# A two-block FFN kernel: the upper part of gate and up weights times both parts of the rows in one product of 512 columns

## The reference, cut to what matters

```python
h = rmsnorm(x, norm_ffn)                      # x: 256 x 1024
x = x + (silu(h @ w_ffn_gate) * (h @ w_ffn_up)) @ w_ffn_down
return rmsnorm(x, norm_final)                 # D_FF = 2816 = 22 tiles of 128
```

## Time and profile before

| | |
|---|---|
| runs | 1421.64, 1420.68, 1421.60 us; median 1421.6 us |
| profiled execution | 1421.5 us, of which its span (first to last instruction) is 1419.7 us |
| busy over the span | PE 77%, PEld 44%, DVE 26%, ACT 21%, POOL 22% |
| chain that ended last | DMA 56%, PE 40% of the span |
| mean granted TensorE clock | 0.893 of full speed |

### The profile page before, as it was taken

One profiled execution on the slowest core, in us unless ns is written; L12 is line 12 of the kernel. 1 busy time (PEld: TensorE's weight loads), 2 busy tenths in 40 slices (PEclk: granted clock), 3 DMA queues, 4 the chain that ended last, 5 costly groups with the idle time before them and its releaser, 6 DMA issues.

```text
span 1419.7 us, 19641 instructions
## 1 busy us (share of the span) xinstructions
PE 1090.4 (77%) x8358; PEld 631.5 (44%) x8358; DVE 366.5 (26%) x723; ACT 304.8 (21%) x449; POOL 312.2 (22%) x216
## 2 busy tenths in 40 slices
PE   7999997656757666666685675666678999999998
PEld 7998732111311211211131121121125987999997
DVE  6686530000100001000010010100004856453343
ACT  5753210000000000000000000000004637454443
POOL 6896000000000000000000000000003787286661
PEclk9999999878777888687877888888799999999999
DMA  9513999999999999999999999999999943475540
GB/s 288 187 34 121 379 426 427 428 427 427 427 428 428 428 428 428 428 429 428 428 428 429 428 428 428 429 428 429 428 427 337 226 137 119 156 246 178 178 149 31
DMA packets 95288, 478.06 MB, mean 337 GB/s; under 512 B 11098, under 2 KB 64217, under 8 KB 70393
## 3 DMA queue, kind: packets, MB, share of 16 engines
q1 hardware_dynamic: 94528, 476.30, 83.4%
q10 hardware_dynamic: 697, 0.84, 0.2%
HBM read 475.88 MB, written 1.25 MB: 336 GB/s over the span
## 4 chain that ended last, share of the span: by engine, by line
DMA 56%; PE 40%; DVE 2%; issue 1%; ACT 1%; SPq 0%; DVEq 0%; ACTq 0%
PE bank L1325 21%; DMA ring<-in_expert_w_up 20%; DMA ring<-in_expert_w_gate 18%; DMA ring<-in_expert_w_down 18%; PE bank L2120 4%; PE bank L1024 4%; PE bank L1046 2%; PE bank L410 1%; PE bank L887 1%; PE bank L427 1%; PE bank L423 1%; DMA cst<-in_shape_consts 0%; PE bank L442 0%; PE bank L438 0%; DVE work L1979 0%
## 5 line engine op out<-in xcount | busy, mean ns | idle before, releaser
L1024 PE MATMUL bank<-ring,work 128*32 128x512 f32 x2000 | 304.2, 741 | 203.1 <-DMA ring<-in_expert_w_up 125.5
L1024 PEld LDWEIGHTS bank<-ring,work 128*32 128x32 f32 x2000 | 60.4, 122 | 436.4 <-DMA ring<-in_expert_w_up 202.6
L1299 POOL TENSOR_TENSOR slot_r<-ring,slot_r 128x512 fp32r<-128x512 f32 (+1 forms) x123 | 227.8, 1880 | 106.8 <-ACT slot_r L1271 106.8
L1308 POOL TENSOR_TENSOR slot_r<-ring,slot_r 128x512 fp32r<-128x512 f32 x16 | 21.9, 1396 | 956.2 <-ACT slot_r L1277 956.2
L1046 PE MATMUL bank<-ring,work 128*32 128x512 f32 x1024 | 154.7, 739 | 80.6 <-DMA ring<-in_expert_w_down 76.4
L1325 PE MATMUL bank<-slot_r 128*128 128x256 f32 (+2 forms) x1080 | 159.5, 287 | 3.8 <-DVE tokm_r L2482 1.8
L1325 PEld LDWEIGHTS bank<-slot_r 128*128 128x128 f32 (+1 forms) x1080 | 144.3, 191 | 7.9 <-issue 5.1
L1098 DVE TENSOR_TENSOR work<-work,bank 128x512 f32<-128x512 f32 x16 | 11.0, 688 | 490.4 <-PE bank L1024 490.4
L1325 PE MATMUL bank<-work_r,slot_r 128*128 128x256 f32 x704 | 129.1, 283 | 0.2 <-DVE chan_r L1847 0.2
L1108 DVE SCALAR_TENSOR_TENSOR hres<-bank,work,hres 128x512 f32<-128x512 f32 x64 | 48.1, 751 | 269.9 <-PE bank L1061 266.9
L1271 ACT ACTIVATE slot_r<-ring 128x2048 fp32r<-128x2048 f32 x62 | 116.6, 1902 | 3.2 <-DMA ring<-in_w_in 3.0
(11 more groups left out here) (418 smaller groups left out, 1045.8 us busy)
## 6 DMA issues: line engine op xcount, KB each, us to landing
ring<-in_expert_w_down SPq DMA_DIRECT2D x64, 2048.0 KB, 35.6
ring<-in_expert_w_gate SPq DMA_DIRECT2D x63, 2048.0 KB, 36.0
ring<-in_expert_w_up SPq DMA_DIRECT2D x62, 2048.0 KB, 35.8
ring<-in_w_in SPq DMA_DIRECT2D x23, 1024.0 KB, 8.2
ring<-in_w_ffn_gate SPq DMA_DIRECT2D x11, 1024.0 KB, 6.1
ring<-in_w_ffn_up SPq DMA_DIRECT2D x11, 1024.0 KB, 5.3
ring<-in_w_ffn_down SPq DMA_DIRECT2D x11, 1024.0 KB, 5.3
ring<-in_w_out SPq DMA_DIRECT2D x8, 1024.0 KB, 4.9
```

Of the source, the lines that this page charges most:

```text
L1024: ins = pe.matmul(bank[b][32 * j:32 * j + 32, :], xg[:, 2 * s + kk, a * CAP:(a + 1) * CAP], w_[kk][:, j * W5:(j + 1) * W5], start=(s == 0 ...
L1299: ins = eng.tensor_tensor(ring_r[s][:, a:a + step], ring[:, s, a:a + step], ring_r[s][:, a + UNIT:a + UNIT + step].bitcast(F32), ALU.subtract)
L1308: ins = eng.tensor_tensor(ring_r[s][:, at:at + q], ring[:, s, at:at + q], ring_r[s][:, at + UNIT:at + UNIT + q].bitcast(F32), ALU.subtract)
```

## The change

1. The upper and lower parts of the rows now lie side by side in `early` (`x3[:, k, 0]`, `x3[:, k, 1]`). A step k is `both_parts`: weights upper x both parts, 512 columns over a whole bank, and weights lower x rows upper, 256 columns into its first half. The second half of a bank holds weights upper x rows lower.
2. So the two halves must be added. For gate and for up, ScalarE copies the second half from PSUM to SBUF (`ffw`), VectorE adds the first half from PSUM to it. Then VectorE multiplies gate by rs, and silu by up; both multiplications now read SBUF alone. A new semaphore `ff_half` counts the copies.
3. Tile 2 has its sums in banks 1 and 2 in place of 4 and 6, and does not wait for `ff_h`; down 0 waits for `ff_h` >= 3 before its first product into bank 1.
4. The final norm's weights are loaded into `flatc`; the semaphores `hn_ready` and `repeat_ready` become one, `pool_made`.

The diff's core (what is left out are the semaphores of point 4 and calls of `upper_parts` and `lower_parts` with the new places):

```diff
-        nf2_bc = poolT[:, :, :].rearrange("p a t -> p (a t)")
+        nf2_bc = flatc[:, 0:D]
...
-        xh = ftile(5, 4, True).rearrange("p (k t) -> p k t", k=DK)
+        x3 = early_r[:, :].rearrange("p (k a t) -> p k a t", k=DK, a=2)
+        ffw = (work(5), work(6))
+
+        def gate_bank(u):
+
+            return 1 if u == 2 else 4 + u % 2
+
+        def up_bank(u):
+
+            return 2 if u == 2 else 6 + u % 2
...
                         for i in range(3):
                             for half in range(2):
+                                if g + f + t + i == 0 and half:
+                                    pe.wait_ge(S.ff_h, 3)
                                 ins = part(f, t, half, (i,))
                 ins.then_inc(S.ff_down_out, 1)
+
+            def both_parts(out_, wh, wl, k):
+
+                pe.matmul(out_[:, :], wh, x3[:, k].rearrange("p a t -> p (a t)"), start=k == 0, stop=False, skip_group_check=True)
+                return pe.matmul(out_[:, 0:T], wl, x3[:, k, 0], start=False, stop=k == DK - 1, skip_group_check=True)
...
-                        ins = three(pe, bank[b][:, 0:T], (w_[0][:, k, 0:P], w_[1][:, k, 0:P]), (xh[:, k, :], chan_r[:, k, :]),
-                                    k == 0, k == DK - 1)
+                        ins = both_parts(bank[b], w_[0][:, k, 0:P], w_[1][:, k, 0:P], k)
...
-                    if u >= 2:
+                    if u > 2:
                         pe.wait_ge(S.ff_h, u - 1)
...
-                            ins = three(pe, bank[b + u % 2][:, 0:T], (wh[:, k, cols_], wl[:, k, cols_]),
-                                        (xh[:, k, :], chan_r[:, k, :]), k == 0, k == DK - 1)
+                            ins = both_parts(bank[b], wh[:, k, cols_], wl[:, k, cols_], k)
...
             for u in range(NFT):
                 g, f = u // FB, u % FB
-                act.wait_ge(S.ff_scaled, u + 1)
+                act.wait_ge(S.ff_g_out, u + 1)
                 if u >= 2:
                     act.wait_ge(S.ff_h, u - 1)
+                act.activation(ffw[u % 2][:, 0:T], bank[gate_bank(u)][:, T:2 * T], ACT.Copy).then_inc(S.ff_half, 1)
+                act.wait_ge(S.ff_scaled, u + 1)
                 act.activation(ffs[u % 2], ffg[u % 2], ACT.Silu).then_inc(S.ff_silu, 1)
+                act.wait_ge(S.ff_u_out, u + 1)
+                act.activation(ffw[u % 2][:, T:2 * T], bank[up_bank(u)][:, T:2 * T], ACT.Copy).then_inc(S.ff_half, 1)
                 act.wait_ge(S.ff_h, u + 1)
...
-                dve.tensor_tensor(ffg[u % 2], bank[4 + u % 2][:, 0:T], rs3_bc, ALU.mult).then_inc(S.ff_scaled, 1)
+                dve.wait_ge(S.ff_half, 2 * u + 1)
+                link(dve.tensor_tensor(ffg[u % 2], ffw[u % 2][:, 0:T], bank[gate_bank(u)][:, 0:T], ALU.add))
+                dve.tensor_tensor(ffg[u % 2], ffg[u % 2], rs3_bc, ALU.mult).then_inc(S.ff_scaled, 1)
...
                 scaled_gate(u)
+                dve.wait_ge(S.ff_half, 2 * u + 2)
+                upper = ffw[u % 2][:, T:2 * T]
+                link(dve.tensor_tensor(upper, upper, bank[up_bank(u)][:, 0:T], ALU.add))
                 dve.wait_ge(S.ff_silu, u + 1)
-                dve.wait_ge(S.ff_u_out, u + 1)
                 if f == 0 and g >= 2:
                     dve.wait_ge(S.ff_down_out, g - 1)
-                dve.tensor_tensor(h_full(g)[:, f], ffs[u % 2], bank[6 + u % 2][:, 0:T], ALU.mult).then_inc(S.ff_h, 1)
+                dve.tensor_tensor(h_full(g)[:, f], ffs[u % 2], upper, ALU.mult).then_inc(S.ff_h, 1)
```

More of the change, by code:

```diff
@@ L169, in build @@
         cst = sb("cst", [P, max(KEEP_W, MASKS_AT + SLOT // 2)])
-        early = sb("early", [P, SLOT])
+        early, early_r = sb_r("early", [P, SLOT])
         qk = early[:, 0:4 * W5].rearrange("p (a h t) -> p a h t", a=2, h=H)
@@ L1168, in mix1_wout @@
             sp.dma_start(rw, io["router_w"].rearrange("o (k p) e -> (o p) k e", p=P)).then_inc(S.wab_in, 16)
-        sems("hn_ready rel_in relrow_out relrow_stored")
-        sems("repeat_ready rows2_evac")
+        sems("pool_made rel_in relrow_out relrow_stored")
+        sems("rows2_evac")
         sems("proj2_out proj2_evac dots_out relu_ready relu_used mask_ready biasmask_ready")
@@ L1549, in second_pe @@
             pe.wait_ge(S.rows2_evac, 2)
-            pe.wait_ge(S.repeat_ready, 1)
+            pe.wait_ge(S.pool_made, 2)
             pe.matmul(bank[1][:, 0:T], repeat, kgw[0:IDX_DIM, :], start=True, stop=True)
@@ L1668, in second_act @@
                 if t == 0:
-                    act.wait_ge(S.hn_ready, 1)
+                    act.wait_ge(S.pool_made, 1)
                 else:
@@ L1793, in second_pool @@
             pool.wait_ge(S.scat_added, 4 * E - 1)
-            pool.tensor_tensor(tokm[:, 0], hres[:, 0], nf_bc, ALU.mult).then_inc(S.hn_ready, 1)
+            pool.tensor_tensor(tokm[:, 0], hres[:, 0], nf_bc, ALU.mult).then_inc(S.pool_made, 1)
             pool.wait_ge(S.slot_used, E * SPE)
@@ L1797, in second_pool @@
             pool.tensor_copy(repeat.rearrange("p (r c) -> p r c", r=4),
-                             ident[0:IDX_DIM, 0:IDX_DIM].unsqueeze(1).to_broadcast([IDX_DIM, 4, IDX_DIM])).then_inc(S.repeat_ready, 1)
+                             ident[0:IDX_DIM, 0:IDX_DIM].unsqueeze(1).to_broadcast([IDX_DIM, 4, IDX_DIM])).then_inc(S.pool_made, 1)
             for n in range(1, 6):
@@ L2025, in second_dve @@
                     if t + half == 0:
-                        lower_parts(dve, "x3", "norm_ffn_2", X3B, xh, chan_r, range(DK // 2))
+                        lower_parts(dve, "x3", "norm_ffn_2", X3B, x3[:, :, 0], x3[:, :, 1], range(DK // 2))
                 if t:
                     split_low(dve, FF_FIRST + 2, True)
-        sems("ff_g_out ff_u_out ff_silu ff_h ff_down_out ff_out out_ready")
+        sems("ff_g_out ff_u_out ff_half ff_silu ff_h ff_down_out ff_out out_ready")
         sems("w_hi w_lo_dve w_lo_pool a_hi a_lo")
@@ L2154, in ff_pe @@
                     u = FB * g + f
-                    if u >= 2:
+                    if u > 2:
                         pe.wait_ge(S.ff_h, u - 1)
                     cols_ = slice(f * P, (f + 1) * P)
-                    for b, (wh, wl), done in ((4, gate, S.ff_g_out), (6, up, S.ff_u_out)):
-                        if u == 1 and b == 6:
+                    for b, (wh, wl), done in ((gate_bank(u), gate, S.ff_g_out), (up_bank(u), up, S.ff_u_out)):
+                        if u == 1 and b == up_bank(u):
                             pe.wait_ge(S.rms_ready, RMS["h3"] + 1)
@@ L2195, in ff_act @@
             squares3(1)
-            upper_parts(act, "x3", "norm_ffn_2", X3B, xh)
+            upper_parts(act, "x3", "norm_ffn_2", X3B, x3[:, :, 0])
             squares3(0)
@@ L2233, in ff_dve @@
         def ff_dve(dve, link):
-            lower_parts(dve, "x3", "norm_ffn_2", X3B, xh, chan_r, range(DK // 2, DK))
+            lower_parts(dve, "x3", "norm_ffn_2", X3B, x3[:, :, 0], x3[:, :, 1], range(DK // 2, DK))
             dve.wait_ge(S.root_ready, ROOT["h3"] + 1)
```

## The result

| kernel | median | runs | ratio to before, 95% interval |
|---|---|---|---|
| before | 1421.2 us | 21 (1420.3 to 1427.3) | |
| changed | 1426.8 us | 21 (1425.0 to 1429.1) | 1.0040 (1.0034 to 1.0046) |

The change makes the kernel slower, as forecast, but by 5.6 us and not by 3.7 us. The profiled execution of the changed kernel has a span of 1424.4 us, 4.7 us more than before. The FFN's part of it, from gate's fifth step in tile 0 (the product that waits for the rows' lower parts) to the end of the last product, took 184.7 us before (1229.31 to 1413.98 us) and takes 189.9 us now (1228.78 to 1418.71 us): 5.3 us more. It begins half a microsecond earlier, and that half microsecond is there long before the FFN (one piece of the chain starts at 1120.68 us before and at 1120.18 us now). The 0.3 us between 5.3 us and the medians' 5.6 us are not traced.

The account below looks back on a forecast made before the run. TensorE was taken to bound the second block's FFN. From 1421.5 us, +5.4 us (down 0's later product), -3.4 us (cheaper products) and +1.7 us (half clock) gave 1425.2 us, range 1422.3 to 1426.9 us.

Parts of the forecast that it names:

- rival 1: At the shared port, tile 2's h comes before GpSimd's next operation and ends 1.0 us earlier: 1424.2 us; chance 0.17.
- rival 3: The port costs the multiplications nothing: 1420.7 us, or 1422.4 us with a clock fall; chance 0.07.
- the clock: After the wait in down 0, TensorE runs 3.41 us at half clock, costing 1.7 us.
- Rival 2: The waits are as worked out, but TensorE's clock stays: 1423.5 us; chance 0.12.
- the term of the products: In gate and up, one wide and one narrow product replace three narrow ones; 18 later tiles save 3.4 us.
- I take 11.9 ns, the row of the same width, type and clock: Saving per gate or up step, 347.8 ns for 359.7 ns, with the wide product priced from the down units.
- The bounds: Saving per gate or up step: nothing if a wide product costs two narrow ones, at most 13.2 ns.
- no later wait: After down 0, TensorE waits no more for h; before down 10, 0.2 us of slack remain.
- Rivals 4 and 5: 4: banks suffice, 1417.4 us, chance 0.04. 5: wide product saves nothing, 1428.6 us, or a third wait appears, chance 0.08.

Follow-up runs that it names:

- e3: Changed kernel with gate's sum and silu written to PSUM, so both multiplications have one PSUM operand: 1423.5 us, ratio 1.0016.
- e2: Changed kernel with 14 unused products of 512 columns on TensorE ahead of the wait in down 0: 1424.7 us, ratio 1.0028.
- e4: Changed kernel with, from tile 1 on, each bank's eight wide products first, then its eight narrow ones: 1425.3 us, ratio 1.0028.
- e1: Changed kernel with the bank part alone undone, tile 2 back in banks 4 and 6, no wait in down 0: 1421.0 us, ratio 1.0002.
- e8: As e7, but from tile 4 on each step makes gate's wide, up's wide, gate's narrow, up's narrow product: 1420.5 us (one run).
- e9: Changed kernel with tiles 0 and 1 and ScalarE's waits there as before, old banks, later tiles wide first with PSUM operands: 1417.1 us, ratio 0.9974.
- e7: Changed kernel with tiles 0 to 3 and banks as before the change, later tiles wide and narrow in turn: 1419.8 us, ratio 0.9994.

## Why the prediction came out as it did

**Right: where TensorE waits.** Waits of 2.0 us before tile 3 and 4.1 us in down 0 were forecast; the profile has 1.8 and 3.8 us from start to start, and down 0's second product begins 5.2 us later in the stretch than before (5.4 us forecast). The way there was right too: the gate multiplications of 0.77, 1.07 and 1.05 us (0.82, 1.10, 1.09 us by the steps), the last one of tile 2 behind GpSimd's next operation at 1.42 us. That multiplication was only 0.12 us behind it; rival 1 was as near as it said. e3 shows the port as the cause, so rival 3 falls.

**Right: the clock.** Half clock for 3.41 us, from 0.6 us after the long wait; 1.6 us by e2, 1.7 us forecast. Rival 2 falls.

**Wrong in size: the term of the products.** The step "I take 11.9 ns, the row of the same width, type and clock" failed. The 227.9 ns were those of wide products among wide ones. In turn with narrow ones a step costs 352.9 ns, 6.8 ns less than before and not 11.9 ns. Over 288 steps that is 1.5 us; the down units behind such tiles cost 5.50 us for 5.47 us, 0.3 us in all. So the term was -1.7 us where I had -3.4 us. e4 shows it: with eight of a kind in a row the term is back (two tiles 11.14 us; 11.13 us forecast). The bounds were 0 and 13.2 ns a step, and the range should have reached to their dear end: the trace had rows of one width in a row and none of a change. 1.7 us is all that the sum lacks for the stretch: +5.4 - 1.7 + 1.7 makes 5.4 us, 5.3 us measured. The ratio 1.0040 of 1421.6 us is 1427.3 us, 0.4 us above the range. The saving of 2.5 ns a step that the prediction works out from the Trainium skill (TensorE: Matmul & The Clock Gate, section "Wait — 56ns, not 53.3ns?") fits neither: 6.8 ns in turn and 11.6 ns grouped were measured.

A count is off too, without weight: 48 products lie between 1229.31 us and the product that spreads rs, so 8 steps of tile 0 follow the wait and not 6. TensorE is the bound for 344 steps, and tile 3 comes 40 steps earlier, not 38: 0.02 us.

**Missed: what the banks do.** The wait in down 0 was sized nearly rightly, and its counterpart, no bank part at all, not looked at. e1 shows that, with the longer chain there, the bank part is the difference between no loss and one of 5.6 us.

**Right: no later wait.** In the changed kernel TensorE never waits after 1255 us. Rivals 4 and 5 fall, 5 with its third wait; its price side (the wide product saves nothing) is too dear: 6.8 ns a step were saved, between it and the forecast's 11.9 ns.

## What to carry to other kernels

Giving a stage other buffers doesn't remove a wait if their owner comes next: it moves the wait to the owner's first use, so ask when that is, and what stands behind it in the order. A chain on slower engines is cheapest to lengthen where they wait for the bound engine and dearest where they already run behind it, as in the first tiles here; there the old form may stay. Take the price of an operation from rows with the same neighbours, and where the trace has none, let the range reach to the other bound.

## What the runs showed of the hardware

All products here are fp32r with new weights for each. A product of 512 columns cost 236.1 ns (start to start) in turn with products of 256 (changed kernel), and 229.7 ns in a run of eight of its own (e4). Two of each in turn cost 347.9 ns for one of each (e8), about as grouped (348.1 ns, e4), and one of each in turn 352.9 ns. A VectorE multiplication of 128x256 with two SBUF operands took 0.77 to 1.42 us beside GpSimd's operations, and 0.42 us with one of the operands in PSUM (e3).

TensorE's granted clock stood at 0.50 for 3.41 us behind a wait of 3.8 us (changed kernel, 0.6 us after the products resumed) and behind one of 2.2 us (e3, 0.8 us after), both from start to start; it stayed at 1.00 behind the one of 1.8 us before tile 3 (changed kernel). Silu's table load of 1.28 us ran ahead of ScalarE's wait when there was one wait (e9, 1233.69 us), and behind the scaling that it waited for when there were two in a row (e7, 1235.89 us). Where it is placed in general no run shows.
